# q and k with the token parts side by side, retention's weighted sums in parts, and a later, denser layer norm in a fused two-block layer

## The reference, cut to what matters

```python
proj = h @ w_in[l]
q, k, v, z_ret, u_val, u_gate, z_conv, g_a, g_b = jnp.split(proj, split_at, axis=-1)
qh = rotary(q...); kh = rotary(k...) * RET_HEAD_QK ** -0.5          # 4 heads of 256
ret = head_groupnorm(retention_chunkwise(qh, kh, vh))                # v: 4 heads of 512
y_a = (ret * jax.nn.silu(z_ret)) @ w_ret_out[l]
a = causal_depthwise_conv_2(u_val * jax.nn.sigmoid(u_gate), conv_w[l], conv_b[l])   # 31 taps
a = jax.nn.silu(layernorm(a, conv_ln_g[l], conv_ln_b[l]))
y_b = (a * jax.nn.silu(z_conv)) @ w_conv_out[l]
y = (jax.nn.sigmoid(g_a) * y_a + jax.nn.sigmoid(g_b) * y_b) @ w_out[l]
x = x + gate * rmsnorm(y, post_norm_g[l])
```

## Time and profile before

| | |
|---|---|
| three runs | 836.94, 838.89, 838.90 us (median 838.89) |
| profiled execution | 837.87 us, of which the span from first to last instruction is 836.1 us |
| TensorE busy | 827.8 us (99%), 5146 matmuls |
| VectorE / ScalarE / GpSimd busy | 731.1 us (87%) / 500.2 us (60%) / 45.4 us (5%) |
| granted TensorE clock, mean | 0.999 |
| read from HBM | 159.20 MB |

### The profile page before, as it was taken

The page is one execution under the profiler, slowest core; times in us unless marked ns, Lnnn a source line. Parts: engine busy times, 40 slices in busy tenths (PEclk is TensorE's granted clock), DMA queues, the critical chain, the costliest instruction groups (busy, mean ns, idle before and its releaser), DMA issues.

```text
span 836.1 us, 13942 instructions
## 1 busy us (share of the span) xinstructions
PE 827.8 (99%) x5146; PEld 725.1 (87%) x5146; DVE 731.1 (87%) x1179; ACT 500.2 (60%) x804; POOL 45.4 (5%) x46
## 2 busy tenths in 40 slices
PE   8999999999999999999999999999999999999997
PEld 8999998789888888888888788998887798888886
DVE  7799899868877898888989979999999999988774
ACT  6899858576566555555565775333346675546743
POOL 0001101341100000000000000000001220000000
PEclk9999999999999999999999999999999999999999
DMA  9875675511875877777776656655454435564531
GB/s 277 256 253 169 211 245 174 146 38 45 278 232 179 261 262 263 257 256 252 238 257 218 221 185 213 202 184 169 155 198 151 152 118 200 186 231 171 188 115 50
DMA packets 129882, 164.13 MB, mean 196 GB/s; under 512 B 17407, under 2 KB 92199, under 8 KB 129703
## 3 DMA queue, kind: packets, MB, share of 16 engines
q1 hardware_dynamic: 129831, 163.45, 59.9%
HBM read 159.20 MB, written 4.23 MB: 195 GB/s over the span
## 4 chain that ended last, share of the span: by engine, by line
PE 98%; DVE 1%; DMA 1%; issue 0%; ACT 0%; DVEq 0%; SPq 0%; ACTq 0%
PE psum L695 16%; PE psum L727 14%; PE psum L728 14%; PE psum L734 14%; PE psum L704 8%; PE psum L677 6%; PE psum L686 6%; PE psum L678 6%; PE psum L1028 2%; PE psum L631 1%; PE psum L641 1%; PE psum L635 1%; PE psum L1033 1%; PE psum L915 1%; PE psum L1146 1%; PE psum L1134 1%
## 5 line engine op out<-in xcount | busy, mean ns | idle before, releaser
L1220 ACT ACTIVATE w_hi<-w_raw 128x1024 fp32r<-128x1024 f32 x255 | 266.6, 1061 | 188.2 <-PE psum L734 87.1
L1786 DVE TENSOR_TENSOR w_lo<-w_raw,w_hi 128x1024 fp32r<-128x1024 f32 x256 | 305.2, 1221 | 44.3 <-ACT w_hi L1220 42.2
L695 PE MATMUL psum<-hT,w_hi 128*128 128x512 f32 x576 | 138.9, 391 | 0.0
L695 PEld LDWEIGHTS psum<-hT,w_hi 128*128 128x128 f32 x576 | 105.4, 188 | 20.2
L727 PE MATMUL psum<-w_hi,hT 128*128 128x512 f32 x280 | 113.3, 405 | 0.0
L728 PE MATMUL psum<-w_hi,hT 128*128 128x512 f32 x280 | 109.3, 390 | 0.0
L2399 DVE SCALAR_TENSOR_TENSOR cv<-aP,par,cv 128x256 f32<-128x256 f32 x240 | 107.9, 519 | 0.0
L677 PE MATMUL psum<-hT,w_hi 128*128 128x256 f32 x432 | 107.4, 286 | 0.0
L678 PE MATMUL psum<-hT,w_hi 128*128 128x256 f32 x432 | 105.9, 283 | 0.0
L677 PEld LDWEIGHTS psum<-hT,w_hi 128*128 128x128 f32 x432 | 82.8, 192 | 0.4 <-issue 0.2
L678 PEld LDWEIGHTS psum<-hT,w_hi 128*128 128x128 f32 x432 | 82.9, 192 | 0.3 <-issue 0.2
(11 more groups left out here) (341 smaller groups left out, 1108.6 us busy)
## 6 DMA issues: line engine op xcount, KB each, us to landing
w_raw<-in_w_in_dram SPq DMA_DIRECT2D x44, 1024.0 KB, 5.1
w_raw<-in_sc_w_in_dram SPq DMA_DIRECT2D x32, 1024.0 KB, 7.9
w_raw<-in_gdn_w_in_dram SPq DMA_DIRECT2D x23, 1024.0 KB, 7.1
ada<-in_w_ada_dram SPq DMA_DIRECT2D x24, 512.0 KB, 4.8
w_raw<-in_gdn_w_out_dram SPq DMA_DIRECT2D x8, 1024.0 KB, 5.5
w_raw<-in_sc_w_out_dram SPq DMA_DIRECT2D x8, 1024.0 KB, 6.4
w_raw<-in_w_ret_out_dram SPq DMA_DIRECT2D x8, 1024.0 KB, 5.1
w_raw<-in_w_conv_out_dram SPq DMA_DIRECT2D x4, 1024.0 KB, 5.1
```

The lines of the kernel that those rows point to most:

```text
L695: pe.matmul(o, w_hi[s][:, k, mine], hT[:, h * KH2 + k, :, :], start=h == 0 and k == 0, stop=False, skip_group_check=True)
L1220: act.activation((w_hi[half_slot(g, h)] if home is None else third_hi[half_slot(g, home)])[:, :, :], raw[slot][:, h * KH2:(h + 1) * KH2, : ...
L1786: return dve.tensor_tensor(o, whole, hi.bitcast(F32), ALU.subtract)
```

## The change

1. **qk** uses `chunk_apart` on TensorE instead of `chunk`: the two activation parts stand side by side as one operand of 512 columns, with one bank for each 128 channels, and the sums come out in two halves that have to be added. ScalarE copies one half out of PSUM, VectorE adds the other to it, and rotates from there. The loop over the chunks is not unrolled on TensorE, so both halves' high products come before both halves' low ones.
2. **Weighted sums** are made in three fp32r products each, from new tiles `st_hi`, `st_lo`, `vt_hi`, `vt_lo`. ScalarE makes the high parts in v, VectorE the low ones; VectorE now reads v's sums last (`READ_BY`).
3. **The gating** with silu(z_ret) moves from GpSimd to VectorE (`gated`).
4. **The convolution's operations** are handed out later: 1 instead of 3 in each step of qk, 8 instead of 9 and 6 or 7 instead of 8 in v, 6 instead of 7 in zret, 8 instead of 4 in the first step of gates, and 12 of them in the first two steps of ret_out.
5. **The layer norm** in ret_out: mean behind chunk 2 instead of 0, variance behind 4 instead of 3, reciprocal in step 5 instead of 4, all silus in step 5 (before: 4 and 5), all products with `zc` and high parts in step 6 (before: 5 and 6), all low parts in step 7 (before: 6 and 7).

```diff
-                        elif name in ("sc_in", "glu"):
+                        elif name in ("sc_in", "glu", "qk"):
                             chunk_apart(i, g0, j, midway if ahead and j == 2 else None)
...
-                pe.wait_ge(st_ready, min(RH, c + 1))
+                pe.wait_ge(st_ready, RH + h + 1)
                 if c >= 4:
                     pe.wait_ge(gn_ready, c - 3)
                 vh = slice(h * RDV, (h + 1) * RDV)
                 o = psum[:, 4 + c % 4, :]
-                mm = pe.matmul(o, st[:, h, t * P:(t + 1) * P], vt[:, 0, vh], start=True, stop=(t == 0))
-                if t:
-                    mm = pe.matmul(o, st[:, h, SEQ:SEQ + P], vt[:, 1, vh], start=False, stop=True)
+                for b in range(t + 1):
+                    cs = slice(t * P, (t + 1) * P) if b == 0 else slice(SEQ, SEQ + P)
+                    pe.matmul(o, st_hi[:, h, cs], vt_hi[:, b, vh], start=b == 0, stop=False, skip_group_check=True)
+                    pe.matmul(o, st_hi[:, h, cs], vt_lo[:, b, vh], start=False, stop=False, skip_group_check=True)
+                    mm = pe.matmul(o, st_lo[:, h, cs], vt_hi[:, b, vh], start=False, stop=b == t, skip_group_check=True)
                 mm.then_inc(ro_done, 1)
...
-                if c == 0:
+                if c == 2:
                     pe.wait_ge(ln_sum_step, 4)
                     pe.matmul(psum[:, 6, 0:SEQ], ones, ln_sum[0][:, 0, :], start=True, stop=True).then_inc(mean_done, 1)
-                if c == 3:
+                if c == 4:
                     pe.wait_ge(ln_sum_step, 8)
                     pe.matmul(psum[:, 7, 0:SEQ], ones, ln_sum[1][:, 0, :], start=True, stop=True).then_inc(var_done, 1)
             wide_deep("ret_out", yT_hi, yT_lo, (y_op_ready, 2 * KT), beside=layer_norm)
...
-            chunks("qk")
+
+            def beside_qk_2(i, j, done):
+                c, g = 4 * i + j, FIRST["qk"]
+                act.wait_ge(half_done, done)
+                act.wait_ge(bank_free, 4 + g + c - 1)
+                act.activation(glu_part[j % 2][:, :, :], psum[:, 2 * j:2 * j + 2, SEQ:2 * SEQ], ACT.Copy).then_inc(sc_act, 1)
+            chunks("qk", beside_qk_2, unroll=True)
...
+            def beside_v(i, j, done):
+                c = 4 * i + j
+                if c >= RH:
+                    act.wait_ge(st_ready, RH)
+                    act.wait_ge(sco_done, RH)
+                    act.activation(st_hi[:, c - RH, :], st[:, c - RH, :], ACT.Copy).then_inc(part_hi_ready, 1)
+                if c % 2:
+                    act.wait_ge(half_done, done)
+                    act.activation(vt_hi[:, :, c // 2 * CW2:(c // 2 + 1) * CW2], psum[:, j - 1:j + 1, :], ACT.Copy).then_inc(part_hi_ready, 1)
+            chunks("v", beside_v, unroll=True)
...
-                if c == 1:
+                if c == 2:
...
-                if c == 3:
+                if c == 4:
                     act.wait_ge(var_done, 1)
                     act.activation(lnm[:, 1, :], psum[:, 7, 0:SEQ], ACT.Sqrt, scale=1.0 / D, bias=eps_n[:, :]).then_inc(ln_step, 1)
-                if c in (4, 5):
-                    for n in range(KH2 * (c - 4), KH2 * (c - 3)):
+                if c == 5:
+                    for n in range(KT):
                         act.wait_ge(lns_ready, n // 2 + 1)
                         act.activation(cv[:, n, :], cv[:, n, :], ACT.Silu, scale=par[:, 1, V_LG + n:V_LG + n + 1],
                                        bias=par[:, 1, V_LB + n:V_LB + n + 1]).then_inc(lna_ready, 1)
-                if c in (5, 6):
-                    for q in range(2 * (c - 5), 2 * (c - 4)):
+                if c == 6:
+                    for q in range(KT // 2):
                         pair = slice(2 * q, 2 * q + 2)
                         act.wait_ge(lnz_ready, q + 1)
-                        act.activation(cT_hi[:, pair, :], cv[:, pair, :], ACT.Copy).then_inc(chi_ready, 1)
+                        act.activation(cT_hi[:, pair, :], cv[:, pair, :], ACT.Copy).then_inc(part_hi_ready, 1)
...
-            for n in range(NT * RH):
-                h, t = n // NT, n % NT
-                pool.wait_ge(gn_ready, n + 1)
-                vh = slice(h * RDV, (h + 1) * RDV)
-                pool.tensor_tensor(vt[:, t, vh], og[t][:, :], zr[:, t, vh], ALU.mult).then_inc(rg_ready, 1)
...
-                conv_share(3)
+                conv_share(1)
                 dve.wait_ge(half_done, done)
-                dve.tensor_tensor(rp1[:, :, :], bank(j), cos2, ALU.mult)
-                dve.tensor_tensor(rp2[:, :, :], bank(j), sin2, ALU.mult).then_inc(bank_free, 1)
+                dve.wait_ge(sc_act, 6 * KT - 2 + COUNT["glu"] - 2 + c + 1)
+                dve.tensor_tensor(ug_sum[:, :, :], psum[:, 2 * j:2 * j + 2, 0:SEQ], glu_part[j % 2][:, :, :], ALU.add).then_inc(bank_free, 1)
                 dve.wait_ge(bank_free, 4 + FIRST["qk"] + c + 1)
+                dve.tensor_tensor(rp1[:, :, :], ug_sum[:, :, :], cos2, ALU.mult)
+                dve.tensor_tensor(rp2[:, :, :], ug_sum[:, :, :], sin2, ALU.mult).then_inc(rp_step, 1)
+                dve.wait_ge(rp_step, 2 * c + 1)
                 dve.tensor_tensor(qkT[:, 2 * c:2 * c + 1, :], rp1[:, 0:1, :], rp2[:, 1:2, :], ALU.subtract)
                 dve.tensor_tensor(qkT[:, 2 * c + 1:2 * c + 2, :], rp2[:, 0:1, :], rp1[:, 1:2, :], ALU.add).then_inc(rp_step, 1)
-                dve.wait_ge(rp_step, c + 1)
+                dve.wait_ge(rp_step, 2 * c + 2)
...
-                conv_share(9 if c < RH else 8)
+                conv_share(8 if c < RH else 6 + c // 7)
                 if c < RH:
                     dve.wait_ge(sco_done, c + 1)
                     dve.tensor_tensor(st[:, c, :], psum[:, 4 + c, 0:3 * P], decay[:, c, :], ALU.mult).then_inc(st_ready, 1)
+                else:
+                    dve.wait_ge(part_hi_ready, PARTS_BY[c - 1] + 1)
+                    part_lo(st_lo[:, c - RH, :], st[:, c - RH, :], st_hi[:, c - RH, :]).then_inc(st_ready, 1)
+                if c % 2:
+                    dve.wait_ge(part_hi_ready, PARTS_BY[c])
+                    columns = slice(c // 2 * CW2, (c // 2 + 1) * CW2)
+                    part_lo(vt_lo[:, :, columns], psum[:, j - 1:j + 1, :], vt_hi[:, :, columns]).then_inc(bank_free, 2)
...
+            def gated(h):
+                vh = slice(h * RDV, (h + 1) * RDV)
+                for t in range(NT):
+                    dve.wait_ge(gn_ready, NT * h + t + 1)
+                    dve.tensor_tensor(vt[:, t, vh], og[t][:, :], zr[:, t, vh], ALU.mult).then_inc(rg_ready, 1)
...
-                conv_share(7)
+                conv_share(6)
...
+                if n and t == 0:
+                    gated(h - 1)
...
                 conv_share(5 if j else 8)
+                if j == 0:
+                    gated(RH - 1)
                 split_two(j)
...
-                conv_share(10 if c else 4)
-                if c == COUNT["gates"] - 1:
+                conv_share(10 if c else 8)
+            chunks("gates", last_pairs, unroll=True)
+
+            def layer_norm(i, j, done):
+                c = 4 * i + j
+                if c < 2:
+                    conv_share(6)
+                if c == 1:
+                    assert not conv_ops
                     dve.wait_ge(cv_step, CW * KT)
                     pair_sum(0, cv[:, KT - 2:KT, :], 2)
                     halves_sum(0, 3)
-            chunks("gates", last_pairs, unroll=True)
-
-            def layer_norm(i, j, done):
-                c = 4 * i + j
-                if c == 0:
-                    assert not conv_ops
-                if c == 1:
+                if c == 2:
                     dve.wait_ge(mean_done, 1)
...
-                if c == 4:
+                if c == 5:
                     dve.wait_ge(ln_step, 1)
...
-                if c in (5, 6):
-                    for q in range(2 * (c - 5), 2 * (c - 4)):
-                        pair = pairs[q]
+                if c == 6:
+                    for q, pair in enumerate(pairs):
                         dve.wait_ge(lna_ready, 2 * q + 2)
                         dve.tensor_tensor(cv[:, pair, :], cv[:, pair, :], zc[:, pair, :], ALU.mult).then_inc(lnz_ready, 1)
-                if c in (6, 7):
-                    for q in range(2 * (c - 6), 2 * (c - 5)):
-                        pair = pairs[q]
-                        dve.wait_ge(chi_ready, q + 1)
+                if c == 7:
+                    for q, pair in enumerate(pairs):
+                        dve.wait_ge(part_hi_ready, 2 * RH + q + 1)
                         part_lo(cT_lo[:, pair, :], cv[:, pair, :], cT_hi[:, pair, :]).then_inc(cop_ready, 1)
```

More of the change, by code:

```diff
@@ L56 @@
 ORDER = [name for name, _ in PHASES]
-READ_BY = {name: "act" if name in ("z", "v", "zret", "zconv", "gates") else "dve" for name in ORDER}
+READ_BY = {name: "act" if name in ("z", "zret", "zconv", "gates") else "dve" for name in ORDER}
 DEEP = ("gdn_out", "sc_out", "ret_out")
@@ L93 @@
 SHIFTED = ((4, 5, 6, 7), (6, 7))
```

(10 more changed lines are left out.)

2 lines of the change are left out of this document (1 added, 1 removed).

## The result

| | before | after |
|---|---|---|
| median, us | 837.6 (6 runs, 836.94 to 838.9) | 847.4 (6 runs, 845.47 to 848.38) |
| ratio to before, 95% interval | | 1.0111 (1.01 to 1.0123) |
| profiled execution: time / span, us | 837.87 / 836.1 | 847.3 / 845.5 |

What follows compares the result with a forecast made beforehand. TensorE, busy in 99% of the span, was taken to bound the kernel. The terms -3.9 + 3.2 + 5.6 + 1.9 = +6.8 us on the profiled 837.87 us gave 844.7 us, range 839.6 to 848.0.

Steps and rivals of the forecast that it cites:

- qk: In qk, TensorE's eight chunks take 5.57 us each instead of 5.76: -1.5 us.
- weighted sums: In zret, nine fp32r products per head replace three float32 ones on TensorE: -2.4 us.
- VectorE late for the mean: Behind chunk 2 of ret_out, TensorE waits for VectorE's sum before the mean's matmul: +3.2 us.
- tail of the layer norm: At the end of ret_out, TensorE waits for the first `cT_lo` before conv_out: +5.6 us.
- clock: Behind the wait at conv_out, TensorE runs twelve passes at half clock: +1.9 us.
- more lag: Rival: low parts and rotation's waits carry 2 to 3 us into gates: 847; chance 0.12 shared with no shortening.
- the parts don't shorten TensorE: Rival: fp32r sums no faster than float32, waits as before: 848; chance 0.12 shared with more lag.
- TensorE's part: In qk and zret, TensorE's work gets shorter: -3.9 us in full if nothing waits.
- GpSimd's price: In zret, GpSimd's gating slows VectorE by 2.1 us for each head; not entered in the sum.
- the clock holds: Rival: the wait at conv_out is there but the half rate behind it isn't: 842.8; chance 0.24.
- VectorE is in time: Rival: no wait for the mean in ret_out, only the tail: 839.6, or 841.5 with the clock; chance 0.14.
- Both waits are hidden: Rival: ScalarE overlaps VectorE more closely in ret_out, the saving stands alone: 834.0; chance 0.10.

Runs made afterwards that it cites:

- e5: e3 with q and k summed in the PSUM banks again, without ScalarE's copies and VectorE's additions: 836.06 us.
- e6: e3 with v and the decayed scores left whole, so the weighted sums are 12 fp32 matmuls instead of 36 fp32r ones: 837.58 us.
- e10: e3 run once more, unchanged, beside e11: 834.59 us.
- e11: e6 run once more, unchanged, beside e10: 837.43 us.
- e3: The changed kernel with the edits of e1 and e2 together: 834.08 us.
- e4: The changed kernel with useless matmuls in both TensorE waits, 4 before the mean's and 8 behind ret_out's last chunk: 843.54 us.
- e1: The changed kernel with VectorE's products with `zc` and low parts of `cT` put ahead of the splits of their steps in ret_out: 838.16 us.
- e2: The changed kernel with 7 instead of 6 convolution operations per zret step, leaving 4 instead of 12 for ret_out: 842.06 us.
- e7: e3 with retention's eight gate products moved back from VectorE to GpSimd: 838.28 us.

## Why the prediction was right, and where it was off

The direction, the two waits and their places were right, and 847.4 lies inside the range. The sum was 3.0 us short of the measured difference. Term by term, in us:

| term | predicted | measured | from |
|---|---|---|---|
| qk | -1.5 | -1.5 | table, before to after; e5 +1.6 |
| weighted sums | -2.4 | -2.4 to -2.8 | table, e6 +2.4; e10 and e11 |
| VectorE late for the mean | +3.2 | +2.7, and +0.8 at `w_lo` | waits; two halves 6.22 in e3, 6.19 in the kernel after |
| tail of the layer norm | +5.6 | +5.7 | waits |
| clock | +1.9 | +3.9 | e4; rows of TensorE |
| sum | +6.8 | +8.8 to 9.2 | |

The spans differ by 9.4, the medians by 9.8. Counted from starts the two waits are 2.85 and 5.91 us, and the sum with the smaller price of the weighted sums is 9.6: in the trace next to nothing stays without a place.

**The step that was off is the clock**, the term that was mis-sized: +1.9 us predicted, +3.9 measured. It was wrong twice. Its count: I gave the half rate to one wait and took the mean's of 3 us as too short to matter, without saying so; the rows show it fall there too, for 1.5 us. Its size: I priced it from twelve passes of 256 columns at the kernel's start, at 0.155 us more for each, though the clock printed there is full, so that no cold pass was seen in them. What is slow here are passes of 512 columns, 0.43 us apart instead of 0.23, and conv_out's first half has twelve of them: 2.4 us. The upper end that I gave, 3.8, comes near, but by luck: it stood for twice as many passes at 0.155. That 847.4 lies in the range is luck in part too. Its upper end, 848.0, was set by "more lag" (847) and "the parts don't shorten TensorE" (848; the sum of its terms, 837.87 + 3.2 + 5.6 + 1.9, is 848.6), and both are wrong. The forecast with its clock term at 3.9 would have been 846.7.

**The layer norm's tail** was worked out from the order of two queues, and each of its links can be laid on the trace. F, chunk 5's first product, starts at 769.80. Predicted and found, from F: reciprocal begins 5.0 and 5.45, first product done 7.45 and 7.9, silus done 11.4 and 12.0, two high parts of weights 13.4 and 13.9, splits 14.8 and 15.35, high parts of `cT` 17.9 and 18.4, splits 21.3 and 21.8, first `cT_lo` 22.0 and 22.4. The lag of 0.4 to 0.6 us is there from the first link on: chunk 5's first half, right behind the variance's matmul, took 772.76 - 769.80 = 2.96 us and not 2.73, and ScalarE's high part began 0.26 us behind it and not 0.03. TensorE asked 16.6 us after F, where 16.35 was said, so that about half of it cancels out of the wait. e1 confirms it from the other side: take VectorE's pieces out from behind the splits, and nothing else, and the wait is gone.

**VectorE late for the mean.** The first product of gates starts at 693.08. The first split was said to come 3.85 us later, the last sum to be done 63.1 later; they came at 697.26 and 756.17 + 0.42, 4.2 and 63.5 later. TensorE was ready for it 60.7 us after the start, where 59.9 was said: it had lost 0.8 at the low part. The steps of gates in the kernel after, against the earlier trace rows:

```profile
703.84 4.04 DVE L2414 SCALAR_TENSOR_TENSOR cv<-aP,par,cv 128x256 f32<-128x256 f32 x10
707.80 2.35 DVE L1801 TENSOR_TENSOR w_lo<-w_raw,w_hi 128x1024 fp32r<-128x1024 f32 x2
...
716.31 1.71 DVE L2411 TENSOR_SCALAR cv<-aP,par 128x256 f32<-128x256 f32 x2
717.95 3.24 DVE L2414 SCALAR_TENSOR_TENSOR cv<-aP,par,cv 128x256 f32<-128x256 f32 x8
```

The steps are 6.23 apart as said, and the one with GpSimd's pair sum (716.31 on) is 0.85 us longer; +1.0 was said. That part of the wait might show a chunk earlier at a low part stood in the prediction, and it did: 0.8 of 3.5. A chunk takes 5.46 us of TensorE and 6.23 of VectorE, so each step of gates loses 0.8 us of the lead. e2 moves eight operations to where there is room, and the wait goes. The room is small: in e3 the sum is done at 751.97 + 0.43 = 752.4, and its matmul starts at 752.92.

**TensorE's part** came out of the rows to a tenth: heads of zret are now 12.92 us apart in the chain of waits, where 12.95 was said and the earlier trace rows had 13.55:

```profile
629.89 0.91 PE psum L737 x4
...
642.81 0.91 PE psum L737 x4
```

The trace's price for qk, 1.5 us, is what e5 shows: 1.6 us between the marks, 2.0 between the medians. The estimate by the Trainium skill ("TensorE: Matmul & The Clock Gate", section "Back-to-back issue gap") was 0.3 us, and the measurement decides against it. **GpSimd's price** on VectorE, 2.1 us for each pair of products, was right too (e7: 4.94 against 2.86 us). That it doesn't enter the sum of this change fits the terms above, and no run tests it by itself.

Of the rivals, "the clock holds" is refuted by the windows, "VectorE is in time" by the wait at the mean. "Both waits are hidden" did not happen; e3 gives about its time, but by another order of VectorE's queue, not by the closer overlap that the rival named. "The parts don't shorten TensorE" is refuted by e5 and e6.

## What to carry to other kernels

A saving on the engine that sets the time is worth its sum only if the engines that feed it keep their lead: here 3.9 us were gained and 13.3 lost again (the spans differ by 9.4), in three waits that come from where operations stand in the queues, and in the clock behind two of them. Reordering the same instructions (e3) won all of it back but the 0.8 us at `w_lo`. When a step is moved, follow each queue in order with its waits, and ask at each wait what stands behind it that is wanted sooner; put what ends the chain ahead of work whose own input is still to come. And price a wait of TensorE with what the clock does behind it: look for each wait, short ones too, and count the passes that follow, at their own size.
